# A hybrid layer and two MLA/DSA/MoE layers: norm rows spread by TensorE, two expert slabs loaded earlier, gather in parts

## The reference

```python
def second_block(x, w_in, q_norm_g, w_q_up, kv_norm_g, w_uk, w_uv, w_o, ln1_g, ln1_b,
              router_w, router_bias, w_gate, w_up, w_down, ln2_g, ln2_b):
    ...
    for l in range(DEPTH_2):                                   # 2 layers
        mix = hybrid_mixer(x, w_in[l], ..., w_o[l], pos, slopes, n_keep)   # MLA heads, then DSA heads
        x = layer_norm(ALPHA * x + mix, ln1_g[l], ln1_b[l])
        ffn = grouped_moe(x, router_w, router_bias, w_gate[l], w_up[l], w_down[l])
        x = layer_norm(ALPHA * x + ffn, ln2_g[l], ln2_b[l])
    return x

def grouped_moe(h, router_w, router_bias, w_gate, w_up, w_down):
    ...                                # 16 experts in 4 groups; the best group, in it the best 2
    hg = jnp.einsum('nd,edf->nef', xt, w_gate)
    hu = jnp.einsum('nd,edf->nef', xt, w_up)
    act = jax.nn.silu(hg) * hu * gates[:, :, None].astype(hg.dtype)
    out = jnp.einsum('nef,efd->nd', act, w_down)
```

## Time and profile before

| | us |
|---|---|
| median of 3 runs | 1145.16 (1140.54 to 1145.2) |
| the profiled execution | 1142.94 |
| its span, first to last instruction | 1141.1 |
| PE busy in it | 1083.8 (95%) |
| DVE / ACT / POOL busy | 565.4 / 438.4 / 92.2 |
| DMA: moved, mean rate | 294.6 MB, 258 GB/s |

### The profile page before, as it was taken

The page is one execution under the profiler, slowest core; times in us unless marked ns, Lnnn a source line. Parts: engine busy times, 40 slices in busy tenths (PEclk is TensorE's granted clock), DMA queues, the critical chain, the costliest instruction groups (busy, mean ns, idle before and its releaser), DMA issues.

```text
span 1141.1 us, 16230 instructions
## 1 busy us (share of the span) xinstructions
PE 1083.8 (95%) x6228; PEld 745.9 (65%) x6228; DVE 565.4 (50%) x1082; ACT 438.4 (38%) x797; POOL 92.2 (8%) x120
## 2 busy tenths in 40 slices
PE   7999998999999999899999999889989999999985
PEld 5898988999998798675344443358867744444332
DVE  5754376767667557747222222274684742222224
ACT  5345455555545345743122111143574521121111
POOL 2200000000000112510000000011252000000000
PEclk9999999999999988999999999999989999999998
DMA  8843255565555333358999999944242999999993
GB/s 293 266 148 112 75 176 191 170 200 165 195 192 174 117 128 114 112 196 352 422 420 421 421 421 421 418 158 125 79 156 72 395 368 421 420 421 421 420 421 129
DMA packets 81717, 294.60 MB, mean 258 GB/s; under 512 B 7268, under 2 KB 40402, under 8 KB 56946
## 3 DMA queue, kind: packets, MB, share of 16 engines
q1 hardware_dynamic: 79168, 287.20, 66.0%
q10 hardware_dynamic: 1682, 4.27, 1.0%
q0 software_dynamic: 800, 2.22, 0.5%
HBM read 292.62 MB, written 1.05 MB: 257 GB/s over the span
## 4 chain that ended last, share of the span: by engine, by line
PE 81%; DVE 8%; DMA 5%; ACT 3%; issue 3%; SPq 0%; DVEq 0%; POOL 0%; ACTq 0%
PE bank L2490 17%; PE bank L2499 9%; PE bank L2021 8%; PE bank L2022 8%; PE bank L2023 8%; DMA moe_w<-in_w_up 5%; PE bank L2082 4%; PE bank L2083 4%; PE bank L2084 4%; PE bank L1946 4%; PE bank L2522 3%; PE bank L2116 3%; PE bank L2477 2%; PE bank L2100 2%; PE bank L2204 1%
## 5 line engine op out<-in xcount | busy, mean ns | idle before, releaser
L1183 DVE TENSOR_TENSOR lo<-raw,hi 128x2048 fp32r<-128x2048 f32 (+3 forms) x78 | 166.9, 2146 | 62.7 <-ACT hi L726 62.4
L726 ACT CAST hi<-raw 128x2048 fp32r<-128x2048 f32 (+3 forms) x78 | 139.5, 1795 | 59.7 <-PE bank L2023 57.4
L1425 DVE TENSOR_TENSOR proj<-bank,proj 64x512 f32<-64x512 f32 x32 | 34.7, 1085 | 197.6 <-PE bank L2512 195.3
L2021 PE MATMUL bank<-hi,xs 128*128 128x512 f32 (+2 forms) x312 | 125.9, 404 | 5.8 <-DVE xs L1217 2.9
L2082 PE MATMUL bank<-xs,hi 128*128 128x256 f32 x448 | 127.8, 285 | 3.6 <-DVE xs L1213 1.5
L2083 PE MATMUL bank<-xs,hi 128*128 128x256 f32 x448 | 126.8, 283 | 0.0
L2084 PE MATMUL bank<-xs,lo 128*128 128x256 f32 x448 | 126.7, 283 | 0.0
L2022 PE MATMUL bank<-hi,xs 128*128 128x512 f32 (+2 forms) x312 | 119.5, 383 | 0.0
L2023 PE MATMUL bank<-lo,xs 128*128 128x512 f32 (+2 forms) x312 | 119.3, 382 | 0.0
L1114 ACT ACTIVATE proj<-bank 64x512 f32<-64x512 f32 x32 | 18.9, 590 | 204.6 <-PE bank L2491 204.6
L2082 PEld LDWEIGHTS bank<-xs,hi 128*128 128x128 f32 x448 | 85.9, 192 | 5.0 <-issue 3.5
(11 more groups left out here) (299 smaller groups left out, 2133.6 us busy)
## 6 DMA issues: line engine op xcount, KB each, us to landing
raw<-in_w_up SPq DMA_DIRECT2D x40, 1024.0 KB, 5.2
raw<-in_w_in SPq DMA_DIRECT2D x28, 1024.0 KB, 5.3
moe_w<-in_w_gate SPq DMA_DIRECT2D x24, 1024.0 KB, 19.0
moe_w<-in_w_up SPq DMA_DIRECT2D x24, 1024.0 KB, 20.4
moe_w<-in_w_down SPq DMA_DIRECT2D x24, 1024.0 KB, 20.2
raw<-in_w_down SPq DMA_DIRECT2D x19, 1024.0 KB, 5.4
raw<-in_w_gate SPq DMA_DIRECT2D x10, 1024.0 KB, 16.0
raw<-in_w_o SPq DMA_DIRECT2D x8, 1024.0 KB, 4.9
```

What stands on the lines that cost most here:

```text
L726: nc.scalar.copy(high(n)[:, 0:size], raw[:, n % RING, 0:size]).then_inc(S["hi_done"], 1)
L1183: tt(low(n)[:, 0:size], raw[:, n % RING, 0:size], high(n)[:, 0:size].bitcast(F32), ALU.subtract).then_inc(S["lo_done"], 1)
L2021: mm(out_, lhs_hi, rhs_hi, start=first, stop=False)
```

## The change

- **Slots.** The first slab, gate half 0 of expert 0, gets a place of its own (`first_slot`, the second half of `xg`, loaded once the DSA attention is done). Slab m >= 1 gets slot (m - 1) % 16, and `wide_a` becomes slot 1, loaded as early as `wide_b`. So 17 slabs are issued before any is used, all on SP's queue; ACT issues none. The condition of the later ones stays `moe_used` >= m - 15.
- **Norm rows.** Gain and shift of the first norm come as two rows of 4 KB (`ln_rows`, at partitions 0 and 32) instead of two broadcasts. PE spreads them into banks 4 to 7 with four one-row f32 matmuls, in the place of `open_acc`, each with two fillers behind it. `kept` reads the banks; the first expert's `add_out` starts the accumulators itself and waits for `ln_scaled`.
- **Gather.** PE opens banks 0 and 1 with zeros and gathers f = 0, 1 in two parts: what needs no `rows_lo(1, 0)`, then the rest. DVE's `rows_lo(1, 0)` moves from before `place` to behind the first slots.
- **Logits.** `heads_low(2)` on DVE moves behind the logits of unit 14.
- DVE no longer waits for `ln_in` before `logits_normed`; one of POOL's semaphores is merged.

```diff
-        moe_slots = [wide_b[:]] + [raw[:, i, :] for i in range(RING)]
+        first_slot = xg[:, 1].rearrange("p e c s -> p (e c s)")
+        moe_slots = [wide_b[:], wide_a[:]] + [raw[:, i, :] for i in range(RING)]
...
                 def moe_load(m, src):
-                    dst = moe_slots[m % MOE_SLOTS].rearrange("p (k n) -> p k n", k=src.shape[1])
+                    i = m - 1
                     if m == 0:
+                        return
+                    elif i < AT_RAW:
                         sp.wait_ge(S["turned_a"], 8 * (layer + 1))
...
-                    elif m == GAIN_SLOT:
-                        return
-                    elif m >= MOE_SLOTS:
+                    else:
                         moe_wait(sp, layer, "moe_used", m - MOE_SLOTS + 1)
-                    sp.dma_start(dst, src).then_inc(S[f"moe_in{m % MOE_SLOTS}"], 16)
+                    if i == AT_ATTENTION:
+                        sp.dma_start(first_slot.rearrange("p (k n) -> p k n", k=4), gate_w[0, 0]).then_inc(S["moe_first"], 16)
+                    dst = moe_slots[slot_of(m)].rearrange("p (k n) -> p k n", k=src.shape[1])
+                    sp.dma_start(dst, src).then_inc(S[f"moe_in{slot_of(m)}"], 16)
...
-                pool.dma_start(ln_gb[:, 0, :], gain.partition_broadcast(P)).then_inc(S["ln_in"], 16)
-                pool.dma_start(ln_gb[:, 1, :], shift.partition_broadcast(P)).then_inc(S["ln_in"], 16)
+                for i, src in enumerate((gain, shift)):
+                    pool.dma_start(ln_rows[32 * i:32 * i + 1, :], src.unsqueeze(0)).then_inc(S["ln_in"], 16)
...
                     silu(e)
-                    if e == 0:
-                        act.wait_ge(S["ln_scaled"], 2 * HALVES * layer + HALVES)
-                        act.dma_start(wide_a[:].rearrange("p (k n) -> p k n", k=2),
...
                 nc.vector.tensor_scalar(route[:, 4, :], picked[:], -ELSEWHERE, ELSEWHERE, ALU.mult, ALU.add)\
                     .then_inc(S["vector_step"], 1)
-                rows_lo(1, 0)
                 w.next("vector_step")
                 w.next("counted")
...
-                    nc.vector.scalar_tensor_tensor(out=x[:, half, part], in0=x[:, half, part], in1=ln_gb[:, 0, part],
+                    nc.vector.scalar_tensor_tensor(out=x[:, half, part], in0=x[:, half, part], in1=bank[4 + c][:],
...
-                    ins = tt(x[:, half, part], x[:, half, part], ln_gb[:, 1, part], ALU.add)
+                    ins = tt(x[:, half, part], x[:, half, part], bank[6 + c][:], ALU.add)
...
                 slots_of(0)
+                rows_lo(1, 0)
                 rows_lo(1, 1)
...
-                    if i == 13:
+                    if i == 14:
                         heads_low(2)
...
                 pe.wait_ge(S["logits_normed"], HALVES * (layer + 1))
-                open_acc()
-                busy(12, bank[2])
+                pe.wait_ge(S["ln_in"], 16 * (4 * layer + 2))
+                for which in range(2):
+                    for c in range(2):
+                        mm(acc[which][c][:], const[32 * which:32 * which + 1, C_ONE:C_ONE + 1].broadcast_to([1, P]),
+                           ln_rows[32 * which:32 * which + 1, 512 * c:512 * (c + 1)], start=True, stop=True)\
+                            .then_inc(S["gains_spread"], 1)
+                        busy(2, bank[2])
+                busy(2, bank[2])
+                for f in range(2):
+                    mm(bank[f][:], zeros[:], zeros[:, 0:1].broadcast_to([P, 512]), start=True, stop=False)
                 w.next("marks_made")
                 w.next("chosen")
...
+                moe_wait(pe, layer, "moe_one_hot", HALVES)
+                pe.wait_ge(S["rows_hi"], 2 * HALVES * layer + HALVES + 1)
+                for f in range(2):
+                    gather_parts(f, ((0, 0), (0, 1), (1, 0)))
+                pe.wait_ge(S["rows_lo"], 2 * HALVES * layer + HALVES + 1)
+                for f in range(2):
+                    gather_parts(f, ((1, 1),), stop=True).then_inc(S["moe_gathered"], 1)
+                pe.wait_ge(S["rows_lo"], 2 * HALVES * layer + 2 * HALVES)
+                for f in range(2, 4):
                     if f == 3:
                         w.next("rounds_known")
                     gather_step(0, f, bank[f])
```

More of the change, by code:

```diff
@@ L82 @@
 SC_DSA = HD ** -0.5
-N_FIRST, N_GAINS, N_CONV, N_TABLES, N_ROUTER = 7, 2, 2, 3, 2
+N_FIRST, N_GAINS, N_CONV, N_TABLES, N_ROUTER = 7, 2, 2, 3, 3
 TAKEN = -3e38
@@ L165 @@
               "moe_xg_ready": 4 * EGROUPS - 2, "moe_xg_odd": 2, "moe_hot_ready": HALVES * EXPERTS}
-MOE_COUNTS |= {f"moe_in{i}": 16 * len(range(i, MOE_SLABS, MOE_SLOTS)) for i in range(MOE_SLOTS)}
+MOE_COUNTS |= {f"moe_in{i}": 16 * len(range(i + 1, MOE_SLABS, MOE_SLOTS)) for i in range(MOE_SLOTS)}
 MOE_COUNTS |= {f"moe_{name}": EXPERTS for name in """silu_done act_gated turned turned_copied map_ready out_high out_ready scattered""".split()}
@@ L296, in build @@
         xg = sb("xg", [P, 2, EPG, DC, SLOTS])
+        with nc.sbuf_tensor("ln_rows", [P, D], F32) as ln_rows:
+            pass
         expert_out = sb("expert_out", [P, 2, 512], F32R)
@@ L386, in build, with slot_of @@
         ring_slots = [moe_w[:, RING * part + i, :] for i in (2, 0, 1) for part in range(2)]
[L387 removed]
+        first_slot = xg[:, 1].rearrange("p e c s -> p (e c s)")
+        moe_slots = [wide_b[:], wide_a[:]] + [raw[:, i, :] for i in range(RING)]
         moe_slots += [attention_slot[:], flat[:, 2 * FFE:2 * FFE + SLAB]] + ring_slots[0:2]
         moe_slots += [xn[:].rearrange("p a n -> p (a n)")] + ring_slots[2:]
[L390 to L392 removed]
+        moe_slots += [q_t[:].rearrange("p h t -> p (h t)"), k_t[:].rearrange("p h t -> p (h t)")]
+        AT_RAW, AT_ATTENTION, AT_RING, AT_XN, AT_REST, AT_QK = 2, 5, 7, 9, 10, 14
+        LATE_SLOTS = (0, AT_RING, AT_RING + 1, AT_QK, AT_QK + 1, AT_XN)
         def last_in_slot(slot):
[L396 removed]
+            return max(range(slot + 1, MOE_SLABS, MOE_SLOTS))
+        def slot_of(m):
+            return (m - 1) % MOE_SLOTS
         def apart_from_ring(n):
@@ L590, in _ @@
                 for i in range(RING if layer + 1 < LAYERS else 0):
-                    moe_wait(sp, layer, "moe_used", last_in_slot(RAW_SLOT + i) + 1)
+                    moe_wait(sp, layer, "moe_used", last_in_slot(AT_RAW + i) + 1)
                     load(b + PER_LAYER + L_IN + i, rows_of(A["w_in_2"][layer + 1], 2 * i, 2, 0, D))
@@ L1468, in experts @@
                 gated_slots(0)
+                w.next("gains_spread", 4)
                 for half in range(HALVES):
@@ L1877, in _ @@
                 turned_odd(1, 1)
-                w.next("ln_in", 32)
                 logits_normed(0)
@@ L2482, in moe_slab @@
                 def moe_slab(m, k_per):
-                    moe_wait(pe, layer, f"moe_in{m % MOE_SLOTS}", 16 * (m // MOE_SLOTS + 1))
-                    return moe_slots[m % MOE_SLOTS].rearrange("p (k n) -> p k n", k=k_per)
+                    if m == 0:
+                        pe.wait_ge(S["moe_first"], 16 * (layer + 1))
+                        return first_slot.rearrange("p (k n) -> p k n", k=k_per)
+                    moe_wait(pe, layer, f"moe_in{slot_of(m)}", 16 * ((m - 1) // MOE_SLOTS + 1))
+                    return moe_slots[slot_of(m)].rearrange("p (k n) -> p k n", k=k_per)
                 def raise_half(to, rows_, gate, up, h):
@@ L2514, in turn_act, with add_out @@
                     return ins
-                def add_out(at):
+                def add_out(at, first=False):
                     for half in range(HALVES):
@@ L2522, in add_out @@
                                 ins = mm(acc[half][c][:], slot_to_token[part, at, half * P:(half + 1) * P],
-                                         expert_out[part, split_, :], start=False, stop=False)
+                                         expert_out[part, split_, :], start=first and split_ == 0, stop=False)
                     return ins
@@ L2556, in scatter_expert, with gather_parts @@
                 def scatter_expert(e):
+                    if e == 0:
+                        pe.wait_ge(S["ln_scaled"], 2 * HALVES * layer + HALVES)
                     moe_wait(pe, layer, "moe_map_ready", e + 1)
                     moe_wait(pe, layer, "moe_out_ready", e + 1)
-                    add_out(e % 2).then_inc(S["moe_scattered"], 1)
-                for f in range(4):
-                    if f % 2 == 0:
-                        pe.wait_ge(S["rows_lo"], 2 * HALVES * layer + HALVES + 1 + f // 2)
+                    add_out(e % 2, first=e == 0).then_inc(S["moe_scattered"], 1)
+                def gather_parts(f, pairs, stop=False):
+                    for c in range(2):
+                        chunk = slice((2 * f + c) * P, (2 * f + c + 1) * P)
+                        for half, part in pairs:
+                            ins = mm(bank[f][:, c * 256:(c + 1) * 256], x_rows[:, part, half, chunk], one_hot[:, 0, half],
+                                     start=False, stop=stop and c == 1)
```

(3 more changed lines are left out.)

29 lines of the change are left out of this document (12 added, 17 removed).

## The result

The changed kernel takes 1153.5 us (median of 5 runs, 1152.3 to 1157.2) against 1143.7 (1140.5 to 1145.2) for the kernel before beside it: ratio 1.0094, 95% interval 1.0076 to 1.0113. It is slower by some 10 us, and the forecast of 1150 lay on the right side. The profiled execution has a span of 1152.0 us against 1141.1.

A forecast was written before the change was run, and what follows sets the result against it. PE was taken to pace the experts, its start released by DVE, with 4.0 us load stall per layer. Terms -4.0 - 1.4 + 1.1 + 2.1 + 5.5 = +3.3, twice +6.6, on 1142.94: 1149.5, rounded to 1150 us; range 1137 to 1155.

The forecast's parts named there:

- (a): Expert weight loads: two more slots gain 4.0 to 5.0 us on PE, removing its 4.0 us stall; -4.0 us per layer.
- (b): Attention's tail: `heads_low(2)` one head later removes PE's wait for turned probabilities; -1.4 us per layer.
- (c): DVE ahead of the first expert: `rows_lo(1, 0)` behind the slots delays `xg`; +1.1 us per layer.
- (d): Router stretch on PE: one-row norm matmuls can't pair between fillers, so the count and `place` come later; +2.1 us per layer.
- (e): Router stretch: one-row matmuls let PE's clock fall to 1.2 GHz, not back before the gather; +5.5 us per layer.
- Rival 1: The clock holds in the router stretch: -2.2 us per layer, 1138.5 us; chance 0.22.
- Rival 2: One-row matmuls cost 2.0 us for eight passes as in the old place, clock held: 1134.5 us; chance 0.12.
- low bound: Low end for the one-row matmuls' price, were the pairs kept (2.0 us for all eight passes): -0.3 us per layer.
- either covers the 4.0 us stall: Loads in the expert stage: a lead of 4.0 us (queue restarts for m18) or 5.0 us removes PE's whole stall.
- Rival 3: The slots' lead isn't gained and the 4.0 us stall stays: 1146.5 us with clock held, 1158 with the fall; chance 0.06.

The follow-up runs named there:

- e5: The changed kernel with spreads over all 128 rows, no fillers among or behind them, and `rows_lo(1, 0)` back ahead of `place`; 1135.5 us, 0.993 of before.
- e6: e5 with slabs 15 and 16 issued only after the first half of expert 0; 1141.7 us, 6.2 more than e5.
- e4: The kernel before with only `heads_low(2)` moved behind the logits of unit 14; 1140.4 us, 0.997 of before.
- e3: The changed kernel with `rows_lo(1, 0)` back ahead of `place`; 1151.3 us, 1.0064 of before.
- e1: The changed kernel with the four norm-row spreads over all 128 rows (zeros in the added rows), same fillers; 1141.3 us, 0.9977 of before.
- e9: The kernel before plus four unused one-row f32 matmuls, two fillers behind each, and two instead of twelve fillers behind `open_acc`; 1158.5 us, 1.0128 of before.
- e8: e5 with one-row spreads, the two row groups in turn, in place of full rows, without fillers; 1135.7 us, 0.9935 of before.
- e2: The changed kernel with the one-row spreads next to each other, row groups in turn, the ten fillers behind; 1142.1 us, 0.9976 of before.
- e10: e5 with the gather of f = 0, 1 whole again, without the openings of banks 0 and 1; 1133.2 us, 0.9914 of before.
- e11: e5 run once more, on the chip of e10; 1134.8 us, 0.9924 of before.
- e7: e5 with slab 16 alone issued only after the first half of expert 0, together with slab 17; 1136.4 us, 0.9 more than e5.

## Why the forecast held, step by step

| step, per layer | forecast | measured | from |
|---|---|---|---|
| (a) two more slots | -4.0 | -3.1 | raise to adding, before and after; on average over all traces -3.4, e5 less e6 -3.7 |
| (b) `heads_low(2)` later | -1.4 | -1.4 | e4, turn to weighing, both layers; half of its medians' 3.5 is 1.7 |
| (c) `rows_lo(1, 0)` behind the slots | +1.1 | +1.1 | `place` to `xg`, 5.29 against 4.23; e3: half of its medians' 2.2, count to first raise 0.6 and 1.1 in the two layers |
| (d) one-row matmuls, unpaired | +2.1 | +1.6 | e1: stretch 6.14 against 3.99, less 0.6 |
| (e) the clock | +5.5 | +5.9 | e1 against the changed kernel |

The 0.6 taken off (d) is `place`, which before came 1.03 us after the count because `rows_lo` still ran, and 0.44 after it in the changed kernel; the forecast put this at 0.7. With these, (c), (d) and (e) together are 8.6 against 8.54 and 8.70 in the traces, and 8.7 by the forecast.

- **(e) carried the sign, and was right.** Its evidence was one place in the trace of before in which fillers behind such matmuls ran at half speed though PE was busy. e1 and e9 show it from both sides: taking away the low rows alone brings 12 us, adding the stretch alone costs 15. All nine traced stretches with one-row spreads that began at the full clock met a fall (both layers of the changed kernel, e3, e8 and e9, layer 0 of e2), and none of the eleven with full rows did. As forecast, the clock wasn't back before the gather: it came at 535.4, inside it. Rival 1 (the clock holds) falls.
- **(d)**: unpaired as said; the changeovers were put at 0.1 us each and took next to nothing, hence 6.14 instead of 6.8 us for the stretch. Rival 2 falls for the changed kernel: the pairs come back only with the spreads side by side (e2), and then eight passes take 2.4 us, where the forecast had put 2.0. Its low bound for that case, -0.3, doesn't fit its own rival 2, which has +0.1: 4.75 - 3.99 - 0.7 = +0.1 is right.
- **`kept`** with gain and shift in PSUM takes 1.40 and 1.29 us for each pair of instructions, before 1.41 and 1.29: nothing, as forecast.
- **(c)** was right with its reason: DVE, not the gather, releases the first raise in the changed kernel, so an operation of DVE that leaves a wait and goes behind it costs its length.
- **(a) is the term that was mis-sized.** The mechanism was right, the loads' stall did shrink, but not by all of it: 0.8 us are left. The step that failed is "either covers the 4.0 us stall". The sum gave 4.0 as the lower bound of the lead by counting one pause, while slab 18 waits for the second half of expert 0. In the changed kernel the rate drops twice:

```profile
544.00:547.00 3.00, 1.00 0.84 292
547.00:549.00 2.00, 1.00 0.91 238
549.00:553.00 4.00, 1.00 1.00 420
553.00:554.00 1.00, 1.00 0.90 328
```

  (2 x (421 - 238) + (421 - 328)) / 421 = 1.1 us in these windows, where the forecast had 1.0 between its two bounds and took the lower, 4.0. By that 3.9 us of lead should be left, and e6 against e5 has 3.7 of it; before against after has 3.1. The 0.6 us between these two are no more than the spread of this length from trace to trace. Where the two slots are there and no slab is held back (the changed kernel, e1, e2, e3, e5, e8, e10, e11, both layers) it takes 212.59 to 214.06 us, mean 213.07; with the old slots (before, e4, e9) 216.36 to 216.76, mean 216.51. So the lead is worth 3.4 us on average where 4.0 were forecast, and what makes the single lengths differ stays open. Rival 3 (no lead) falls by e6.
- **The remainder.** Per layer the terms as measured give +4.1, twice 8.2; the spans differ by 10.9. Part of the other 2.7 us probably are low stretches of the clock at other places of this execution, with nothing changed there; their cost wasn't read. The largest that before doesn't have, in windows of after and of before:

```profile
183.80:190.60 6.80, 5.98 (x29) 0.50 0.01 2
```

```profile
183.80:190.60 6.80, 6.66 (x53) 1.00 0.14 20
```

  e1 and e4 have this stretch too, the one with and the other without the norm rows on PE, so it says nothing of the change. The medians lie 9.7 us apart. The forecast of +6.6 on the profiled execution was low by 2 x 0.9 for (a); that it came out within 4 us of the median is owed in part to small misses that offset each other, (d) against (e).

## What to carry to other kernels

A matmul with one row of weights that is used to spread a row is best given all 128 rows (zeros elsewhere) when full-speed work follows: it takes the same time per pass, and here the clock held. What it gives up is the pairing (3.70 against 2.41 us for the eight passes), and where PE waits for another engine behind it anyway, as in e8, it brings 0.6 us a layer and not 5.9. When such work replaces fillers, count its length against the fillers and drop as many; and when a slab of lead is bought, check that the load behind it can be issued before it has arrived, since a slab that goes out alone gives back part of its lead (here the second slab brought 1.2 to 1.5 of its 2.49 us).

## What the runs showed of the hardware that was not expected

- PE busy 13.70 of 13.70 us at a granted clock of 0.50, twice in one execution. And 2.4 us of one-row matmuls went with 6.8 us of low clock in layer 0 of e2 and in both layers of e8. In layer 1 of e2 it was 10.3 us, and the clock had fallen before they began, so there something else took part.
- A low clock can also come in ahead of the spreads. In layer 1 of e7 the clock, 1.00 until 898.0, is at 0.50 from 898.2, 0.3 us before the first of the eight full-height passes (window, then timeline), and it is back at 901.6, while they still run. So the eight take 5.22 us instead of 3.70:

```profile
898.20:898.40 0.20, 0.20 (x2) 0.50 1.07 451
```

```profile
898.48 5.22 PE L2465 MATMUL bank<-ln_rows,const 128*128 128x512 f32 x8
```

  In the other eleven stretches with full rows (e1, e5, e6, e10 and e11 in both layers, e7 in layer 0) the clock didn't fall. What lies ahead of the stretch is the same program in all of them; why this one differs stays open.
- The one-row matmuls at the end of a layer were left as they are. The fillers behind them ran at the low clock in the kernel before; whether full rows pay there was not tried.
